# A two-layer decoder trunk: long and short matmuls by twos in the first block of each turn, a first weight block in halves, a quarter of the last norm on TensorE

## What is computed

```
def _layer_norm(x, g, b):
    mean = jnp.mean(x32, axis=-1, keepdims=True)
    var = jnp.mean(jnp.square(x32 - mean), axis=-1, keepdims=True)
    return ((x32 - mean) * lax.rsqrt(var + LN_EPS) * g + b).astype(x.dtype)

for layer in range(DEPTH):
    ...
    x = _layer_norm(DEEPNORM_ALPHA * x + y, ln_g[layer, 0], ln_b[layer, 0])
    x = _layer_norm(DEEPNORM_ALPHA * x + _sqrelu_mlp(x, mlp_w1[layer], mlp_w2[layer]),
                    ln_g[layer, 1], ln_b[layer, 1])
```

## Time and profile before

| | us |
|---|---|
| three runs | 2142.0, 2144.07, 2140.47 |
| median of them | 2142.0 |
| the profiled execution's own time | 2144.91 |
| its span | 2143.1 |
| TensorE (PE) busy | 2122.6 (99%) |
| VectorE (DVE) busy | 1306.1 (61%) |
| ScalarE (ACT) busy | 973.7 (45%) |
| DMA, mean | 190 GB/s |

### The profile page before, as it was taken

One profiled execution on the slowest core, in us unless ns is written; L12 is line 12 of the kernel. 1 busy time (PEld: TensorE's weight loads), 2 busy tenths in 40 slices (PEclk: granted clock), 3 DMA queues, 4 the chain that ended last, 5 costly groups with the idle time before them and its releaser, 6 DMA issues.

```text
span 2143.1 us, 30984 instructions
## 1 busy us (share of the span) xinstructions
PE 2122.6 (99%) x10948; PEld 1807.5 (84%) x10948; DVE 1306.1 (61%) x1240; ACT 973.7 (45%) x1085; POOL 29.8 (1%) x22
## 2 busy tenths in 40 slices
PE   9999999999999999999999999999999999999997
PEld 8898888888888888888888888888888888888886
DVE  6769665665645554565766666676655545645556
ACT  5595444434434443443544445344434434434442
POOL 0000010000000000000100000010000000000000
PEclk9999999999999999999999999999999999999999
DMA  8666666666566666656555556665666566566664
GB/s 278 190 186 198 222 207 182 190 191 191 179 198 184 194 188 195 186 187 187 167 165 168 164 165 220 196 200 181 195 193 187 186 196 186 177 202 181 194 192 133
DMA packets 210481, 406.13 MB, mean 190 GB/s; under 512 B 12480, under 2 KB 18880, under 8 KB 209376
## 3 DMA queue, kind: packets, MB, share of 16 engines
q1 hardware_dynamic: 210112, 402.90, 60.5%
q10 hardware_dynamic: 288, 2.10, 0.3%
HBM read 402.85 MB, written 2.10 MB: 189 GB/s over the span
## 4 chain that ended last, share of the span: by engine, by line
PE 97%; DVE 1%; issue 1%; ACT 0%; DMA 0%; SPq 0%; DVEq 0%; ACTq 0%
PE ps L368 40%; PE ps L358 34%; PE ps L359 17%; PE ps L591 1%; PE ps L589 1%; PE ps L590 1%; PE ps L499 0%; PE ps L604 0%; PE ps L472 0%; PE ps L471 0%; PE ps L470 0%; PE ps L579 0%; DVE bnst L1047 0%; DVE f L1040 0%; DMA f<-in_x_dram 0%
## 5 line engine op out<-in xcount | busy, mean ns | idle before, releaser
L840 DVE TENSOR_TENSOR wl<-wst,wh 128x1024 fp32r<-128x1024 f32 x744 | 903.1, 1223 | 665.2 <-ACT wh L622 663.2
L622 ACT ACTIVATE wh<-wst 128x1024 fp32r<-128x1024 f32 x744 | 783.0, 1059 | 909.6 <-PE ps L368 469.4
L358 PE MATMUL ps<-xin,wh 128*128 128x512 f32 x3072 | 1088.6, 399 | 1.8 <-issue 1.3
L359 PE MATMUL ps<-xin,wl 128*128 128x256 f32 x3072 | 862.6, 281 | 0.0
L358 PEld LDWEIGHTS ps<-xin,wh 128*128 128x128 f32 x3072 | 577.3, 188 | 145.0 <-issue 1.7
L368 PE MATMUL ps<-wh,hid 128*128 128x512 f32 x2560 | 694.9, 389 | 0.0
L359 PEld LDWEIGHTS ps<-xin,wl 128*128 128x128 f32 x3072 | 580.4, 189 | 0.2
L368 PEld LDWEIGHTS ps<-wh,hid 128*128 128x128 f32 x2560 | 479.9, 188 | 99.4
L368 PE MATMUL ps<-wl,hid 128*128 128x512 f32 x1280 | 404.5, 389 | 0.0
L368 PEld LDWEIGHTS ps<-wl,hid 128*128 128x128 f32 x1280 | 240.3, 188 | 50.0
L850 DVE TENSOR_TENSOR e<-e,ps 128x1024 f32<-128x1024 f32 x32 | 39.1, 1221 | 50.2 <-ACT e L631 50.2
(11 more groups left out here) (114 smaller groups left out, 651.2 us busy)
## 6 DMA issues: line engine op xcount, KB each, us to landing
wst<-in_mlp_w_dram SPq DMA_DIRECT2D x512, 512.0 KB, 3.8
wst<-in_moba_w_qkv_dram SPq DMA_DIRECT2D x96, 512.0 KB, 4.3
wst<-in_rg_w_in_dram SPq DMA_DIRECT2D x64, 512.0 KB, 4.4
wst<-in_rg_w_out_dram SPq DMA_DIRECT2D x32, 512.0 KB, 4.8
wst<-in_moba_w_out_dram SPq DMA_DIRECT2D x32, 512.0 KB, 4.6
gate<-in_ln_g_dram SPq DMA_DIRECT2D x3, 1024.0 KB, 8.1
gate<-in_ln_b_dram SPq DMA_DIRECT2D x3, 1024.0 KB, 10.1
f<-in_x_dram SPq DMA_DIRECT2D x8, 256.0 KB, 8.2
```

The source lines that it names most:

```text
L358: pe.matmul(dst[:, n, :], wh[:, s, w], src[:, c, :, :], start=(c == 0), stop=False)
L359: mm = pe.matmul(dst[:, n, 0:T], wl[:, s, w], src[:, c, 0, :], start=False, stop=(c == NC - 1))
L622: act.activation(wh[:, off % SPLITS, :], wst[:, kb, :], ACT.Copy).then_inc(wh_done, 1)
L840: dve.tensor_tensor(wl[:, off % SPLITS, :], wst[:, off % BLOCKS, :], wh[:, off % SPLITS, :], ALU.subtract).then_inc(wl_done, 1)
```

## The change

Three things are changed.

1. In the first block (kb = 0) of each of the 48 weight-stationary turns, the sixteen matmuls go long, long, short, short (n and n+1 together) where they went long, short, long, short. Each bank still gets its own in the same order.
2. The first weight block is loaded, rounded and subtracted in two halves, one for each chunk c. The first turn starts when the first half is ready (`first_lo`). The transposes of x pair 1, which stood ahead of the turn, now stand between chunk 0 and chunk 1 of it (`opening`); two of the small matmuls on ones fall away, the three behind pair 0 stay.
3. In the last norm, columns 0 to 511 are left to TensorE and ScalarE. VectorE multiplies them by the gain once they are complete, in the second to last pair of turns (`q_ready`). When a half's mean and rstd are known, VectorE makes shift = -mean * rstd (one value per token), ScalarE makes two 128x128 diagonal matrices, diag(rstd) and diag(shift), and TensorE adds identity * bias + diag(rstd) * (x gain) + diag(shift) * gain in PSUM, all in plain float32; ScalarE copies the 512 columns out. VectorE's two passes keep three groups of four. The group of these columns is stored last in each half. The rows of gain and bias for this norm are loaded by ScalarE's queue, ahead of its last W1 turns, instead of by SP behind the last weights.

```diff
             for kb in range(BLOCKS):
...
-                load_block(first[kb], kb, None)
+                if kb == 0:
+                    for q, landed in enumerate((first_half, stage_full[0])):
+                        sp.dma_start(wst[:, 0, q * COLS:(q + 1) * COLS], first[0, :, q, :]).then_inc(landed, 16)
+                else:
+                    load_block(first[kb], kb, None)
...
-            load_rows(3)
             for h in range(HALVES):
-                for g in range(NG):
-                    sp.wait_ge(out_done, h * NG + g + 1)
+                for g in (1, 2, 3, 0):
+                    if g:
+                        sp.wait_ge(out_done, h * (NG - 1) + g)
+                    else:
+                        sp.wait_ge(out_act, h + 1)
...
+            one_by_one = [(n, low) for n in range(GROUP) for low in range(2)]
+            by_twos = [(n, low) for m in range(0, GROUP, 2) for low in range(2) for n in (m, m + 1)]
...
-                    pe.wait_ge(wl_done, b + kb + 1)
+                    if opening and kb == 0:
+                        pe.wait_ge(first_lo, 1)
+                    else:
+                        pe.wait_ge(wl_done, b + kb + 1)
                     for c in range(kb * KCH, (kb + 1) * KCH):
+                        if opening and c == 1:
+                            opening()
+                            pe.wait_ge(wl_done, 1)
                         s = c // KCH % SPLITS
-                        for n in range(GROUP):
+                        for n, low in (by_twos if kb == 0 else one_by_one):
...
-            for k in range(AHEAD_X):
-                input_pair(k)
-                keep_warm(3 - k)
-            between = {k - AHEAD_X + 1: lambda k=k: input_pair(k) for k in range(AHEAD_X, BLOCKS)}
-            turn(xin, 0, B_U, R_X, {**between, BLOCKS - 1: parameters})
+            input_pair(0)
+            keep_warm(3)
+            between = {k - 1: lambda k=k: input_pair(k) for k in range(2, BLOCKS)}
+            turn(xin, 0, B_U, R_X, {**between, BLOCKS - 1: parameters}, opening=lambda: input_pair(1))
...
+            def output_sums(free):
+
+                pe.wait_ge(psum_free, free + 1)
+                pe.wait_ge(rows_loaded, 32 * 4)
+                pe.wait_ge(q_ready, 1)
+                for h in range(HALVES):
+                    pe.matmul(ps[:, h, :], ident[:, :], bias_row[:, 0:COLS], start=True, stop=False)
+                for h in range(HALVES):
+                    pe.wait_ge(diag_ready, 2 * h + 2)
+                    pe.matmul(ps[:, h, :], diag[:, h, 0, :], res[:, h, 0:COLS], start=False, stop=False)
+                    pe.matmul(ps[:, h, :], diag[:, h, 1, :], gain_row[:, 0:COLS], start=False, stop=True)\
+                      .then_inc(out_sum, 1)
...
+            def output_half(h):
+                act.wait_ge(out_shift, h + 1)
+                for k, factor in enumerate((rstd, shift)):
+                    act.activation(diag[:, h, k, :], ident[:, :], ACT.Copy, scale=factor[:, h:h + 1])\
+                       .then_inc(diag_ready, 1)
...
                 if n == 3:
+                    output_half(1)
+                    for h in range(HALVES):
+                        act.wait_ge(out_sum, h + 1)
+                        act.activation(res[:, h, 0:COLS], ps[:, h, :], ACT.Copy).then_inc(out_act, 1)
                     return
...
-                    dve.wait_ge(rows_loaded, 32 * 4)
-                    for g in range(NG):
+                    for g in range(1, NG):
                         dve.scalar_tensor_tensor(out=res[:, h, cols_for(g)], in0=res[:, h, cols_for(g)],
                                                  scalar=mv[:, h, 0:1], in1=gain_row[:, cols_for(g)],
                                                  op0=ALU.subtract, op1=ALU.mult).then_inc(out_link, 1)
-                    inverse(h)
-                    for g in range(NG):
-                        dve.wait_ge(out_link, NG * h + g + 1)
+                        if g == 1:
+                            inverse(h)
+                            dve.scalar_tensor_tensor(out=shift[:, h:h + 1], in0=mv[:, h, 0:1], scalar=-1.0,
+                                                     in1=rstd[:, h:h + 1], op0=ALU.mult, op1=ALU.mult)\
+                               .then_inc(out_shift, 1)
+                    for g in range(1, NG):
+                        dve.wait_ge(out_link, (NG - 1) * h + g)
...
+                    if n == 3 and t == 0:
+                        dve.wait_ge(rows_loaded, 32 * 4)
+                        dve.wait_ge(ln_stat, 8 * n + HALVES)
+                        dve.tensor_tensor(res[:, :, cols_for(0)], res[:, :, cols_for(0)],
+                                          gain_row[:, cols_for(0)].unsqueeze(1).to_broadcast([P, HALVES, COLS]),
+                                          ALU.mult).then_inc(q_ready, 1)
```

More of the change, by code:

```diff
@@ L138, in build_trunk @@
         gain_row, bias_row = gate[:, 0:D], gate[:, D:2 * D]
+        diag = f2[:, 0:4 * P].rearrange("p (h k n) -> p h k n", h=HALVES, k=2)
         norm_t = f3[:, :].rearrange("p (c t) -> p c t", t=T)
-        std, rstd = tok[:, 0, :], tok[:, 1, :]
+        std, rstd, shift = tok[:, 0, :], tok[:, 1, :], tok[:, 2, :]
         stage_full = [sem(f"stage_full{s}") for s in range(BLOCKS)]
+        first_half = sem("first_half")
+        first_hi = sem("first_hi")
+        first_lo = sem("first_lo")
         x_loaded = [sem(f"x_loaded{k}") for k in range(BLOCKS)]
@@ L203, in build_trunk @@
         out_link = sem("out_link")
+        q_ready = sem("q_ready")
+        out_shift = sem("out_shift")
+        diag_ready = sem("diag_ready")
+        out_sum = sem("out_sum")
+        out_act = sem("out_act")
         out_done = sem("out_done")
@@ L343, in _, with turn @@
         def _(pe):
-            def turn(src, half, b, ready, between={}):
+            one_by_one = [(n, low) for n in range(GROUP) for low in range(2)]
+            by_twos = [(n, low) for m in range(0, GROUP, 2) for low in range(2) for n in (m, m + 1)]
+            def turn(src, half, b, ready, between={}, opening=None):
                 dst = banks(half)
@@ L352, in turn @@
                     pe.wait_ge(pair_ready, ready + (kb + 1))
[L353 removed]
+                    if opening and kb == 0:
+                        pe.wait_ge(first_lo, 1)
+                    else:
+                        pe.wait_ge(wl_done, b + kb + 1)
                     for c in range(kb * KCH, (kb + 1) * KCH):
+                        if opening and c == 1:
+                            opening()
+                            pe.wait_ge(wl_done, 1)
                         s = c // KCH % SPLITS
[L356 removed]
+                        for n, low in (by_twos if kb == 0 else one_by_one):
                             w = slice(c % KCH * COLS + n * P, c % KCH * COLS + (n + 1) * P)
[L358 to L360 removed]
+                            if low:
+                                mm = pe.matmul(dst[:, n, 0:T], wl[:, s, w], src[:, c, 0, :],
+                                               start=False, stop=(c == NC - 1))
+                            else:
+                                pe.matmul(dst[:, n, :], wh[:, s, w], src[:, c, :, :], start=(c == 0), stop=False)
                     mm.then_inc(mm_done, 1)
@@ L508, in last_pair @@
                 if n == 3:
+                    output_sums(free)
                     return
@@ L638, in _ @@
                 act.activation(xin[:, k * KCH:(k + 1) * KCH, 0, :], xt_bank(k), ACT.Copy).then_inc(xt_hi, 1)
-                split_hi(0, 0, k)
+                if k == 0:
+                    for q, (landed, done) in enumerate(((first_half, first_hi), (stage_full[0], wh_done))):
+                        act.wait_ge(landed, 16)
+                        act.activation(wh[:, 0, q * COLS:(q + 1) * COLS], wst[:, 0, q * COLS:(q + 1) * COLS],
+                                       ACT.Copy).then_inc(done, 1)
+                else:
+                    split_hi(0, 0, k)
             def conv_hi_part(g):
@@ L742, in last_pair @@
                     splits(b, no, BLOCKS, BLOCKS + 3)
+                if n == 3:
+                    output_half(0)
                 act.wait_ge(ln_var, 2 * n + 2)
@@ L793, in mlp @@
                 s = SLABS - 1
+                if n == 3:
+                    act.wait_ge(prepped, NG * (n + 1))
+                    for dst, src in ((gain_row, ln_g), (bias_row, ln_b)):
+                        act.dma_start(dst, src[1, 1:2, :].to_broadcast([P, D])).then_inc(rows_loaded, 16)
                 w1_turns(s)
@@ L857, in _ @@
                    .then_inc(pair_ready, 1)
-                split_lo(0, k)
+                if k == 0:
+                    for q, (copied, done) in enumerate(((first_hi, first_lo), (wh_done, wl_done))):
+                        half = slice(q * COLS, (q + 1) * COLS)
+                        dve.wait_ge(copied, 1)
+                        dve.tensor_tensor(wl[:, 0, half], wst[:, 0, half], wh[:, 0, half], ALU.subtract)\
```

(3 more changed lines are left out.)

6 lines of the change are left out of this document (1 added, 5 removed).

## The result

The changed kernel takes 2127.14 us (2125.64 to 2128.62, four runs), the kernel before 2143.03 beside it: ratio 0.9927, 95% interval 0.9914 to 0.9940, or 15.9 us less. I had forecast 2140.3, with 2137.4 as the lower end of the range. The two profiled executions lie further apart than the medians: 2144.91 before and 2126.73 after, with spans of 2143.1 and 2124.8.

The account below looks back on a forecast made before the run. TensorE, busy 99% of the span, was taken as the bound in the middle, the weights' low part at the opening, VectorE at the end. -1.2 + 1.05 - 1.55 = -1.7 us from 2142.0 gave 2140.3, range 2137.4 to 2144.2.

Parts of the forecast that it names:

- Part 1: First block of each W1 turn: order by twos saves 25 ns per turn, over 48 turns -1.2 us.
- The bounds: Limits for the order by twos in the first blocks: nothing (0), -2.4 us, or a loss of +1.2.
- the three rates: W1 turns: 353.3 ns per alternating pair, 226.7 per long among long, 120.3 per short among short matmuls.
- order would be worth nothing: Rival for the W1 turns: the gap depends on columns alone; -0.5 us in all, 2141.5; chance 0.11.
- Part 2: Opening: first matmul 0.75 us earlier, but block 1 starts at 12.4 instead of 11.35; +1.05 us.
- The cover: Opening: block 1's load lands at 9.2, ScalarE takes it at about 9.9; the added issue costs nothing, otherwise 0.5 us.
- The rival with the clock still low: Opening: TensorE's clock still low in chunk 0, so the opening costs +2.9 us, time 2142.1; chance 0.27.
- Part 3: Last norm: VectorE ends 2.2 us earlier, a quarter goes to TensorE and ScalarE; -1.55 us.
- The sum: Whole kernel: -1.2 + 1.05 - 1.55 = -1.7 us, forecast 2140.3 us.

Follow-up runs that it names:

- The alone-run: The kernel before with only the order by twos in the first block of each turn: 2129.57 us, ratio 0.9939.
- three groups: The changed kernel with by twos for only the first three groups of four matmuls of a turn: 2135.20 us, ratio 0.9957; with the first two, 2131.14 us, 0.9940.

## Why the prediction was wrong

**Part 1, the step that failed:** "A pair has two switches ... and by twos four matmuls have two switches instead of four: 6.3 ns less per two pairs", in the first block alone, -1.2 us. The price was measured rightly: alternating cost 6.3 to 6.6 ns a pair more than its parts. What it was put down to was wrong. It is no price of a switch but of the long rhythm, and the same instructions also run in a short one without it. The first block sets the rhythm of the 56 pairs behind it. In the turns measured, the block by twos itself takes 0.041 us less than its like before (2786 for 2827 ns; 0.025 forecast), and the seven blocks behind it, for which the step has nothing, 0.054 each. The alone-run gave -13.3 where this step says -1.2, and the run with by twos everywhere came out 2.6 slower than the change by the medians where this step wants -8.4. The bounds fell with it: I had taken the block by twos as the only place where anything could change, and the three rates as stationary. That they differ by under 2% was no argument against a larger effect, since 6.3 ns on each of the 3072 pairs are 19.4 us. Had I looked at the intervals to the nanosecond, a period of three pairs with a spread of 232 to 240 would have told me that 353.3 is a mean over a pattern and not the price of anything.

By the Trainium skill, "TensorE: Matmul & The Clock Gate", section "Back-to-back issue gap", the formula for the gap has the number of columns alone in it. By it order would be worth nothing; these traces have one sequence of columns at 346.7 and at 353.3 ns a pair at the same granted clock, and the measurement decides.

**Part 2, the opening, mechanism right, one cover wrong.** Block 1 was forecast at 12.4 and came at 12.28, the wait ahead of it at 1.3 and came at 1.06, the loss at 1.05 and came at 0.93. But "The added DMA issue ... costs nothing" was wrong: x pair 1 landed at 8.4, 1.7 later than before, and the transposes waited for it [0.19 above]. It did little harm only since chunk 0 was still running. Weight block 1 was late too, issued at 2.70:

```profile
wst<-in_rg_w_in_dram SPq DMA_DIRECT2D x1, 512.0 KB, 7.1
```

So it landed at 9.8, where I had 9.2, and ScalarE began its high part at 9.82, 0.63 behind the start of x pair 1's copy; where the weights were there in time it was 0.49 (5.15 to 5.64 in the kernel before). The cover was used up, at a cost of about 0.14. That block 1 came so near to the forecast is in part luck: the transposes began at 8.49 instead of 8.8, and from there to block 1 it took 3.79 instead of 3.6. The first matmul was also earlier than I had it (6.87 for 7.35), since x pair 0 was transposed from 3.65 on and not from 4.00. That is no chance either: in all eleven profiles with the halves it is 3.57 to 3.77, in the four without 4.00 to 4.16. The rival with the clock still low (2.9, block 1 at 14.3) turned out to be real in five of the other profiles, at 13.4 to 13.6: its price was too high by 0.7 to 0.9. Its condition, that the rise waits for the work of pair 1's transposes, does not hold: in the changed kernel's profiles the full clock begins at 5.57 and 5.72, ahead of them.

**Part 3, the end, right.** -1.55 forecast, -1.9 measured. VectorE ends 2.5 us earlier in relation to its first addition (12.1 us instead of 14.6) where I had 2.2; ScalarE's copy ends 0.1 behind it, as forecast; the last store is issued a third of a microsecond later and lands 2.9 later, where I had allowed 3.05. The two remaining parts together, -0.5 by my sum, are -1.0 in the changed kernel's profile (0.93 - 1.90), and no run tells their sum apart from nothing by its time (no change: 0.9986 to 1.0005 with both of them alone).

**The sum** without part 1's rhythm would have been near: 0.9 of opening, -1.9 of the end. It missed by the 42 turns of 0.4 us.

## What to carry to other kernels

When a loop of unequal matmuls runs at more than the sum of what each takes among its likes, look at the intervals from start to start one by one: a pattern with a period is a rhythm, and one permutation ahead of the loop may move it into a shorter one, for all of the loop. Try the smallest permutations and count, in the trace, how many turns each moves; don't expect that more of it is better (here three groups were no better than two, and by twos everywhere was no better than in the first block). And splitting a transfer in two can delay the next one in its queue by more than the added issue takes (here 0.7 to 2.0 us for 0.47).

## What the runs showed of the hardware

- TensorE alternating 512- and 256-column matmuls (each with its own weight load) has two stable rhythms, 346.7 and 353.3 ns a pair, at one clock. Which it takes depends on what came ahead: behind 384 equal matmuls plain order fell into the long one in both profiles that have it there, twelve times of twelve, and either rhythm was kept for as long as the alternation went on, over ends of turns too (turns 1 to 3 of the kernel with the two other parts alone ran in the short one, without a group by twos anywhere). Behind waits and transposes it can come out either way, so the turns behind them differ from execution to execution. The short rate also has a second pattern: turn 29 of that kernel alternates 230 and 117 ns. What inside the engine holds the phase isn't shown by any run here.
- Groups of two long and two short matmuls run at 348.3 ns a pair, with intervals that alternate between two forms (such as 232, 231, 113, 120 and 233, 236, 116, 112), 695 to 698 ns a group.
- Loading the first 512 KB in two halves let the next transfer in the queue land 0.7 to 2.0 us later (at 7.5 to 8.6 instead of 6.6 to 6.8), with 0.47 of that in the issue. The 256 KB ahead of it landed sooner, 2.8 to 3.0 us behind its issue instead of 3.2 to 3.4. Why the delay is more than the issue was not tried.
- TensorE's clock rose from its lower to its upper level at 5.3 to 8.6 us in nine executions, and at 10.1 to 11.3 in six, all of these with the changed loads. In the changed kernel it rose at 5.57, before the transposes of x pair 1; in the kernel before at 7.40, in the middle of them. The trace's record of the full clock begins at these times, and the starts of the matmuls change pace with it (matmuls on ones 0.21 apart, then 0.11; four transposes in 1.04 or 0.60 us).
